# Recurrent inputs in two halves of the feature sum, recurrent gates of all chunks in one stretch

## What is computed

```
sh1, sc1, g1, sh2, sc2, g2 = split(mod, 6)            # mod = silu(c) @ w_ada + b_ada
z = (x * (1 + sc1) + sh1) @ w_in + b_in               # 11 groups of 512 columns: r_x, r_g, g_q, ...
xc = dwconv(r_x)                                      # 4 taps
r = sigmoid(blockdiag(xc, w_a) + b_a); i = sigmoid(blockdiag(xc, w_x) + b_x)
log_a = -8 * r * softplus(-lam); a = exp(log_a)
u = sqrt(max(-expm1(2 * log_a), 0)) * (i * xc)
h = scan(a, u) from h0                                # forward and backward
y_r = gelu(r_g) * (h_forward + h_backward)
```

## Time and profile before

| what | us |
|---|---|
| median of 3 runs | 844.13 |
| lowest, highest of them | 837.72, 1221.33 |
| the profiled execution | 838.96 |
| its span, first to last instruction | 837.1 |
| TensorE busy in the span | 690.7 (83%) |
| VectorE busy | 563.2 (67%) |
| ScalarE busy | 427.4 (51%) |

### The profile page before, as it was taken

The page is one execution under the profiler, slowest core; times in us unless marked ns, Lnnn a source line. Parts: engine busy times, 40 slices in busy tenths (PEclk is TensorE's granted clock), DMA queues, the critical chain, the costliest instruction groups (busy, mean ns, idle before and its releaser), DMA issues.

```text
span 837.1 us, 12054 instructions
## 1 busy us (share of the span) xinstructions
PE 690.7 (83%) x4619; PEld 548.9 (66%) x4619; DVE 563.2 (67%) x795; ACT 427.4 (51%) x587; POOL 55.9 (7%) x92
## 2 busy tenths in 40 slices
PE   2789989488889989989996169999999999999400
PEld 1487878477777779774445157878888878888300
DVE  2488494965757545652645529999989999998265
ACT  1454687412312435641003038888888888888220
POOL 5300000100000000023000300000000000000020
PEclk9789999789999999999995569999999999999755
DMA  9999887866353353239409857999999999993141
GB/s 322 375 370 400 328 288 247 307 234 240 134 202 136 117 175 129 101 35 237 185 3 370 344 212 268 398 396 397 400 401 400 398 398 397 398 399 140 57 172 50
DMA packets 91681, 221.01 MB, mean 264 GB/s; under 512 B 3287, under 2 KB 3567, under 8 KB 91631
## 3 DMA queue, kind: packets, MB, share of 16 engines
q1 hardware_dynamic: 84320, 197.14, 63.2%
q0 software_dynamic: 6928, 23.07, 8.8%
q10 hardware_dynamic: 383, 0.13, 0.1%
HBM read 180.96 MB, written 39.36 MB: 263 GB/s over the span
## 4 chain that ended last, share of the span: by engine, by line
PE 70%; DVE 9%; ACT 7%; DMA 5%; issue 5%; SPq 2%; POOL 2%; POOLq 0%; DVEq 0%; ACTq 0%
PE ps L1024 66%; DMA ring<-in_w_in 3%; SPq L466 2%; PE ps L1373 2%; ACT w_hi L717 1%; PE ps L1392 1%; DVE w_lo L1522 1%; DMA arena<-slot_outs,arena 1%; POOL slot_rows L645 1%; ACT arena L815 1%; POOL arena L655 1%; DVE arena L1605 1%; ACT arena L812 1%; PE ps L1349 1%; DMA slot_rows<-arena 0%
## 5 line engine op out<-in xcount | busy, mean ns | idle before, releaser
L1888 DVE TENSOR_TENSOR w_lo<-ring,w_hi 128x1024 fp32r<-128x1024 f32 x96 | 114.9, 1221 | 15.7 <-ACT w_hi L925 14.6
L1888 DVE TENSOR_TENSOR w_lo<-arena,w_hi 128x1024 fp32r<-128x1024 f32 x96 | 115.0, 1220 | 9.2 <-ACT w_hi L925 8.2
L925 ACT ACTIVATE w_hi<-ring 128x1024 fp32r<-128x1024 f32 x96 | 100.9, 1063 | 18.9 <-PE ps L1024 18.8
L925 ACT ACTIVATE w_hi<-arena 128x1024 fp32r<-128x1024 f32 x96 | 101.1, 1064 | 15.0 <-PE ps L1024 14.9
L1024 PE MATMUL ps<-h_hi,w_lo 128*128 128x384 f32 x288 | 103.1, 358 | 2.5 <-issue 1.3
L1024 PE MATMUL ps<-w_hi,slot_tokens_lo 128*128 128x512 f32 x256 | 103.7, 405 | 1.4 <-DVE slot_tokens_lo L1895 1.4
L1024 PE MATMUL ps<-w_hi,slot_tokens_hi 128*128 128x512 f32 x256 | 101.1, 395 | 0.0
L1024 PE MATMUL ps<-w_lo,slot_tokens_hi 128*128 128x512 f32 x256 | 100.7, 393 | 0.0
L1024 PE MATMUL ps<-h_hi,w_hi 128*128 128x384 f32 x288 | 98.6, 342 | 0.0
L1024 PE MATMUL ps<-h_lo,w_hi 128*128 128x384 f32 x288 | 98.6, 342 | 0.0
L1024 PE MATMUL ps<-arena 128*32 128x32 f32 (+5 forms) x1576 | 61.6, 234 | 25.7 <-DVE arena L1625 13.1
(11 more groups left out here) (312 smaller groups left out, 1038.1 us busy)
## 6 DMA issues: line engine op xcount, KB each, us to landing
slot_rows<-arena SPq DMA_DIRECT2D x12, 2048.0 KB, 18.6
ring<-in_w_in SPq DMA_DIRECT2D x11, 2048.0 KB, 9.1
ring<-in_w_ada SPq DMA_DIRECT2D x10, 2048.0 KB, 9.6
ring<-in_w_gate SPq DMA_DIRECT2D x8, 2048.0 KB, 14.9
ring<-in_w_up SPq DMA_DIRECT2D x8, 2048.0 KB, 14.9
...
```

The costliest lines, as they stand in the source:

```text
L925: act.activation(w_hi[:, at_ % 4, :], raw[:, q * QUARTER:(q + 1) * QUARTER], ACT.Copy).then_inc(S["hi_ready"], 1)
L1888: tt(w_lo[:, at_ % 4, :], raw[:, q * QUARTER:(q + 1) * QUARTER], w_hi[:, at_ % 4, :].bitcast(F32), ALU.subtract).then_inc(S["lo_dve"], 1)
```

## The change

The list gets another order in its first third, and three places follow from it.

1. Of the x transposes only the first half of the features comes ahead of `ada_col 0` and `2` and `h 0`. Then `first` (all four rx units' high and low parts), then a new job `part q k0 k1`: the rx inputs of chunk q over feature blocks k0 to k1, left open in bank 3 + q. Parts 0 to 2 over k 0 to 3, `ada_row 1`, part 3, `ada_col 1`, `ada_row 3`, `ada_col 3`, `h 1`, parts over k = 4 and 5; `chan rx` does k = 6 and 7 only.
2. SP asks for rx ahead of the early pieces, which lie in free parts of the arena now, in five transfers.
3. `lru_mm c` does both directions into banks 3, 4, 6, 7 in one go, and the four come one after another between the gq inputs. R and I have a buffer for each chunk (units 10, 13, 8 and 9, the latter two being those of mq and mk, whose takes wait for the scans). `rows_ln`, `rows2` and `cT` come later, `lru_scan 3` comes behind `diag`, and nine small instructions of VectorE move from ahead of `h 0` into `sp`. `cT` uses one bank.

```diff
-    steps += [("xT", i, half) for i in range(1, NT) for half in range(2)]
-    steps += [("ada_col", 0), ("ada_col", 2), ("h", 0), ("ada_row", 1), ("ada_row", 3), ("ada_col", 1), ("first",), ("ada_col", 3), ("h", 1)]
+    steps += [("xT", i, 0) for i in range(1, NT)] + [("ada_col", 0), ("ada_col", 2), ("h", 0)] + [("xT", i, 1) for i in range(1, NT)]
+    steps += [("first",)] + [("part", q, 0, 4) for q in range(3)] + [("ada_row", 1), ("part", 3, 0, 4), ("ada_col", 1), ("ada_row", 3), ("ada_col", 3)]
+    steps += [("h", 1)] + [("part", q, k, k + 1) for k in (4, 5) for q in range(4)]
...
-    steps += [rx[0], ("sp",), rx[1], ("conv", 0), rx[2], ("conv", 1), rx[3], ("conv", 2), ("gates",)]
...
+    steps += [rx[0], rx[1], ("conv", 0), rx[2], rx[3], ("conv", 1), ("gates",), ("sp",), ("conv", 2)]
+    steps += [gq[0], ("lru_mm", 0), ("conv", 3), ("rows1",), gq[1], ("lru_mm", 1), gq[2], ("lru_mm", 2), gq[3], ("lru_mm", 3), ("lru_act", 0), ("lru_den", 0)]
...
+    steps += [mq[0], ("prep", 1, 0), ("prep", 1, 1), mq[1], ("prep", 1, 2), ("prep", 1, 3), ("qfb",), mq[2], ("diag",), ("lru_scan", 3), ("ada_row", 6)]
...
-        early = [place(f"early_piece{n}", o_conv + PIECE * n, PIECE).rearrange("p (k n) -> p k n", k=KD) for n in range(2)]
+        early_at = [[(0, 6, 6 * U), (6, 8, 2 * U)], [(0, 6, 13 * U), (6, 7, 2 * U + 1024), (7, 8, 11 * U + 512)]]
...
-        R_, I_ = [[unit(u, off, 768) for u in (10, 13)] for off in (0, 768)]
+        R_, I_ = [[unit(u, off, 768) for u in (10, 13, 8, 9)] for off in (0, 768)]
...
+                    piece(n, win_v[:, :, WIN_COL[name] * G:(WIN_COL[name] + 1) * G], KD)
                     if n == 2:
                         early_piece(0)
                         early_piece(1)
-                    piece(n, win_v[:, :, WIN_COL[name] * G:(WIN_COL[name] + 1) * G], KD)
...
+                    if g in ("mq", "mk") and c == 0:
+
+                        act.wait_ge(S["lru_done"], 3 if g == "mq" else C)
...
                     w = weights(UNIT[job])
-                    for k in range(KD):
+                    for k in range(6 if g == "rx" else 0, KD):
...
+                elif kind == "part":
+                    _, q, k0, k1 = job
+                    if (q, k0) == (0, 0):
+                        pe.wait_ge(S["banks_cleared"], 1)
+                    w = weights(q)
+                    for k in range(k0, k1):
+                        if q == 0:
+                            pe.wait_ge(S["h_lo"], k + 1)
+                        mm3(ps[:, 3 + q, 0:T], [x[:, k, :] for x in w], [x[:, k, :] for x in (HH, HL)], k == 0, False)
...
+                    else:
+                        pe.wait_ge(S["gates_taken"], 4 * c)
+                    pe.wait_ge(S["rx_conv"], c + 1)
+                    for d in range(2):
+                        for g in range(2):
+                            last = mm(ps[:, 3 + 3 * d + g, 0:T], w_bd[d][:, g, c, :], chunk(XC, c))
+                        last.then_inc(S["gates_ready"], 1)
                 elif kind == "diag":
                     pe.wait_ge(S["hg_start"], 1)
+                    pe.wait_ge(S["gates_taken"], 4 * C)
```

More of the change, by code:

```diff
@@ L105, in schedule @@
+    steps += [("h", 1)] + [("part", q, k, k + 1) for k in (4, 5) for q in range(4)]
     u = {g: [("tok", g, q) if g in ("gi", "mv") else ("chan", g, q) for q in range(4)] for g in WIN_ORDER}
     rx, gq, gff, gfb, mq, mk, rg, gi, mv, go, mo = [u[g] for g in WIN_ORDER]
-    steps += [rx[0], ("sp",), rx[1], ("conv", 0), rx[2], ("conv", 1), rx[3], ("conv", 2), ("gates",)]
-    steps += [gq[0], ("conv", 3), ("rows1",), gq[1], ("rows_ln",), ("lru_mm", 0, 0), gq[2], ("lru_mm", 0, 1), ("rows2",), gq[3], ("lru_mm", 1, 0)]
@@ L111, in schedule @@
-    steps += [gff[0], ("lru_mm", 1, 1), ("cT",), ("lru_act", 0), ("lru_den", 0), gff[1], ("lru_act", 1), ("lru_den", 1), ("lru_sqrt", 0), ("lru_sqrt", 1)]
-    steps += [gff[2], ("lru_scan", 0), ("bulk", "gq"), ("ada_row", 4), gff[3], ("lru_mm", 2, 0), ("ada_col", 4), ("lru_scan", 1), ("bulk", "gff")]
-    steps += [gfb[0], ("lru_mm", 2, 1), ("mod", 4), ("prep", 0, 0), ("prep", 0, 1), gfb[1], ("lru_mm", 3, 0), ("prep", 0, 2), ("prep", 0, 3)]
-    steps += [gfb[2], ("lru_mm", 3, 1), ("lru_act", 2), ("lru_den", 2), ("ada_row", 5), gfb[3], ("lru_act", 3), ("lru_den", 3), ("ada_col", 5)]
@@ L115, in schedule @@
-    steps += [("lru_sqrt", 2), ("lru_sqrt", 3), ("bulk", "gfb"), ("lru_scan", 2), ("mod", 5)]
-    steps += [mq[0], ("lru_scan", 3), ("prep", 1, 0), ("prep", 1, 1), mq[1], ("prep", 1, 2), ("prep", 1, 3), ("qfb",), mq[2], ("diag",), ("ada_row", 6)]
+    steps += [rx[0], rx[1], ("conv", 0), rx[2], rx[3], ("conv", 1), ("gates",), ("sp",), ("conv", 2)]
+    steps += [gq[0], ("lru_mm", 0), ("conv", 3), ("rows1",), gq[1], ("lru_mm", 1), gq[2], ("lru_mm", 2), gq[3], ("lru_mm", 3), ("lru_act", 0), ("lru_den", 0)]
@@ new lines, in schedule @@
+    steps += [gff[0], ("lru_act", 1), ("lru_den", 1), ("rows_ln",), gff[1], ("lru_sqrt", 0), ("lru_sqrt", 1), ("bulk", "gq"), ("lru_scan", 0), ("ada_row", 4)]
+    steps += [gff[2], ("lru_scan", 1), ("ada_col", 4), gff[3], ("bulk", "gff"), ("lru_act", 2), ("rows2",), ("lru_den", 2), ("mod", 4)]
+    steps += [gfb[0], ("prep", 0, 0), ("prep", 0, 1), ("lru_act", 3), ("lru_den", 3), gfb[1], ("cT",), ("prep", 0, 2), ("prep", 0, 3), ("ada_row", 5)]
+    steps += [gfb[2], ("lru_sqrt", 2), ("lru_sqrt", 3), ("ada_col", 5), ("lru_scan", 2), gfb[3], ("bulk", "gfb"), ("mod", 5)]
@@ L199 @@
         _key = _job[:2] if _width > 1 else _job
-        _mine = [(_bank + _i) % _banks for _i in range(_width)]
+        _own = _job[:2] == ("chan", "rx")
+        _mine = [3 + _job[2]] if _own else [(_bank + _i) % _banks for _i in range(_width)]
         Z_BANK[_key] = _mine
@@ L213 @@
         TAKEN[_key] = LAST_IN[_mine[-1]]
-        _bank = (_bank + _width) % _banks
+        if not _own:
+            _bank = (_bank + _width) % _banks
 USED = []
@@ L776, in _ @@
                 elif kind == "first":
-                    hi_to(0)
+                    hi_to(3)
                 elif kind == "tok":
@@ L1145, in _ @@
                         x = EARLY_ADA.index(job[1])
-                        pe.wait_ge(early_in[x], 16)
-                        w = early[x]
+                        pe.wait_ge(early_in[x], 16 * len(early_at[x]))
+                        w = [arena[:, at_ + (k - k0) * G:at_ + (k - k0 + 1) * G] for k0, k1, at_ in early_at[x] for k in range(k0, k1)]
                     else:
@@ L1150, in _ @@
                         full(p)
-                        w = slot(p, KD)
+                        w = [slot(p, KD)[:, k, :] for k in range(KD)]
                     for r in range(2):
```

79 lines of the change are left out of this document (37 added, 42 removed).

## The result

The changed kernel takes 848.83 us in the median of its seven runs, the kernel before 842.97 in the median of its seven on the same chip. The ratio is 1.0078, with a 95% interval of 1.0044 to 1.0112: slower by about 6 us, less than 2%, but more than the measurement leaves open. The profiled execution took 847.57 us, its span 845.8 where it was 837.1. The profile of the kernel before (838.96 us) lies 4.0 us under its median, that of the changed kernel 1.3 us, so times read from the two profiles differ by more than the medians do.

The account below looks back on a forecast made before the run. It took TensorE to bound most of the stretch before diag, then VectorE's list to set the end. Start -3.4 and second half +8.4, mostly absorbed, left +0.9 on 838.96: 840 us, range 832 to 850.

Parts of the forecast that it names:

- The base: Starting time to which the forecast added its difference: the profiled execution's 838.96 us, near the low end of three runs.
- The start of rx: Head: rx lands earlier and its first matmul starts at 40.2 us instead of 43.58, a gain of 3.4 us.
- The second half: Head: second modulation at 57.1 us instead of 43.39, rx ending at 69.7 instead of 64.7, a loss of 5.0 us.
- ScalarE's row: Middle: ScalarE copies `ada_row 4` only at 123.2 us; TensorE waits 6.3 us, was 2.15; without it 1.9 us come back.
- VectorE's list: Before diag: gapless VectorE work of 30.1 us from 139.1 to the product's end at 169.2, against 168.4 before.
- Behind the product: After the first product: 9.1 us of VectorE work, `lru_scan 3` included, hides under TensorE's 10.3 us, 1.2 to spare.
- the new waits ... nothing: Behind the product: added waits are for work done 154 to 175 us, before their turn or within 3 us of it.
- a block: Everything behind the first level of scores shifts together, with no change of its own.
- the sum: Start -3.4, second half +8.4, partly absorbed by TensorE's waits and VectorE's end: up to +0.9 at diag and behind it.
- The slower one: 847 us: clock stays at 1.2 GHz for 10 us after three TensorE restarts, 7 us passed on in full; chance 0.18.
- The faster one: 834 us: the head doesn't lose, rx ends near 65 and all shifts by 5 to 6 us; chance 0.22.

Follow-up runs that it names:

- a_old_head: Changed kernel with the order of steps up to `h 1`, early pieces and nine small instructions of the kernel before; 844.08 us, ratio 1.0023.
- a_head2: Changed kernel with ada rows and columns 1 and 3 ahead of most first-half rx matmuls, parts 2 and 3 behind `h 1`; 837.18 us, ratio 0.9948.
- b_new_head: Kernel before with only the changed kernel's order up to `h 1`, its early pieces, banks and nine moved instructions; 853.75 us, ratio 1.0133.
- a_hout_late: Changed kernel with GpSimd's store of the final recurrent state h_fin issued behind the load of C0; 844.78 us, ratio 1.0042.
- a_store_pieces16: Changed kernel with the h_fin store at its place but written in 256 pieces of 16 bytes, not 1024 of 4; 845.58 us, ratio 1.0039.
- b_pool_late: Kernel before with GpSimd's mv bias, S0 and h_fin store also waiting for the first level's state; 846.32 us, ratio 1.0039.
- with the old head: Changed kernel with the kernel before's order up to `h 1` and the h_fin store behind C0's load; 838.75 us, ratio 0.9964.

## Why the prediction was wrong, point by point

- **The base.** 840 was the profiled execution's 838.96 plus 0.9; the median of the kernel before is 842.97. Of the 9.0 us between 839.86 and 848.83, 4.0 are this choice and 5.0 are the change. And I took 17 us as the least that could be told from none; with these runs 0.8% can be.
- **The start of rx** was to be at 40.2 and is at 39.03: right. The 4 us of low clock behind it are there (0.50 in 39.03:43.00).
- **The second half** was to start at 57.1, TensorE to wait 56.9 to 59.9, rx to end at 69.7. It is 56.35, a wait of 3.10 to 59.20, and 69.93. a_old_head and a_head2 show that the reason was the right one: give up or mend that order, and 4.6 or 10.9 us come back by the ratios. But I called the loss 5 us, the end of rx, while the last low half of h, on which VectorE's list hangs, is 13 us later; b_new_head shows what that is worth where nothing hides it.
- **ScalarE's row** and the wait at `ada_col 4`, 6.3 us forecast, 6.27 measured; that almost nothing comes back without it: right as well.
- **VectorE's list** was to run from 139.1 to a product end at 169.2. It ran from 140.69 (lru_act 2 ends 1.1 us later) to 170.71. Off by 1.5 us.
- **Behind the product** is the step that failed. I had the scan hidden with 1.2 us to spare and "the new waits ... nothing", and took what comes behind as a block. The scan is hidden. But three transfers of GpSimd wait for it, and I didn't list them: a step that moves takes with it every transfer that waits for its semaphore. At 159.50 they lay in TensorE's idle 13 us with SP's queue empty behind them; at 176.59 they meet the weight piece, and the store's pieces of 4 bytes hold up its packets and the instructions of TensorE. By the ratios this is 3.0 us (a_hout_late), 3.3 (a_store_pieces16), 3.3 (b_pool_late) and 5.0 (with the old head); in the profiles it is 2.2 to 3.7 us between the second groups of level 0 and 1. Together with the 2.4 us at diag, where the sum had 0.8, that comes near the 5.9 us between the medians.
- **Low clock behind diag**: the stretch 173.40:176.70 is at 0.52 in the changed kernel,

```profile
173.40:176.70 3.30, 3.30 (x28) 0.51 (x18) 3.09 (x7) 0.00 (x0) 0.10 (x1) 0.52 0.01 4
```

  while before the low clock was over after 3.5 us (171.00:177.00 at 0.93). With it go the 0.9 us more between diag and level 0 (11.1 us, forecast 10.3), as in the 14 profiles above. A small term, missed.
- **The rivals.** The slower one (847, low clock of 10 us at the restarts) has nearly the right time for the wrong reason: the clock was low for 4.3, 4.6 and 5.6 us at the three restarts, and not for 10. The faster one is out. No rival had the transfers.
